# Seven products of quarters instead of eight in 39 weight blocks of a fused transformer kernel, and feed-forward groups of 6 and 4 tiles

## The chip, the core and the metric

The kernel runs on one core of a Trainium2 chip (trn2). A core has five engines with a queue each: TensorE (PE in the profile) multiplies matrices, VectorE (DVE) and ScalarE (ACT) work on elements, GpSimd (POOL) too, and SyncE (SP) issues most of the DMA transfers. Every engine does its own instructions in the order in which they were written, and the engines wait for each other through semaphores. The metric is the time of one execution on the device, in microseconds; the median of three runs was 2053.11 us (2051.51 to 2055.26).

## The reference

One transformer block of width 1024 over 512 tokens, then a second block that reads its output. All is fp32. What matters here are the three feed-forward networks, one in the first block ("ff" below) and two in the second ("ff1", "ff2"):

```python
def rmsnorm(x, g):
    y = x * lax.rsqrt(jnp.mean(x * x, axis=-1, keepdims=True) + EPS)
    return y * g

def swiglu(h, w1, w3, w2):
    return (jax.nn.silu(h @ w1) * (h @ w3)) @ w2

# first block: attention of two kinds with gates, then
h = rmsnorm(x, norm_mlp_g)
x = x + jnp.square(jax.nn.relu(h @ w_ff1)) @ w_ff2            # 1024 -> 4096 -> 1024   ("ff")
x = x + sigmoid(rmsnorm(x, norm_ple_g) @ w_ple_gate) * (p @ w_ple)
x = rmsnorm(x, final_norm_g)
# second block
x = x + 0.5 * swiglu(rms_norm(x, norm_ffn1), w1, w3, w2)      # 1024 -> 2816 -> 1024   ("ff1")
x = x + hybrid_mixer(rms_norm(x, norm_mix), ...)              # retention and differential attention
x = x + memory_attention(rms_norm(x, norm_mem_q), mem_n, ...)
x = x + 0.5 * swiglu(rms_norm(x, norm_ffn2), w1, w3, w2)      # ("ff2")
return rms_norm(x, norm_out)
```

## The kernel before

**Three matmuls for one product.** Each fp32 operand is split into two numbers that TensorE takes in one pass: `hi`, the value rounded to the format fp32r, and `lo`, the rest. A product is then three matmuls that add up in a PSUM bank, hi·hi, lo·hi and hi·lo (lines L612, L615, L618, where the weight is the stationary operand; L621, L624, L627, where the tokens are). Activations lie feature by feature: a tile is 128 features by 512 tokens, and a matmul of a weight tile (128x128) with it is 512 columns wide.

**Blocks.** All weights pass in blocks of 256 columns by 8 row tiles, 1 MB, through two buffers in turn (`b % 2`). For block b SyncE transfers the raw weights into `RAW[b % 2]` (`sp_weights`, L665) as soon as the block two before it has given up that buffer; ScalarE rounds them, chunk by chunk of 512 numbers for each partition, into `WH[b % 2]` (`act_weights`, L643), and VectorE subtracts to give the rest in `WL[b % 2]` (`dve_weights`, L652). An ordinary block has 4 chunks and 48 matmuls (2 output tiles, 8 row tiles, 3 each).

**The feed-forward networks.** `plan_ffn` cuts the hidden features into groups of 8 tiles (the last of ff1 and ff2 has 6). A "way up" block makes two hidden tiles of w1 (or w3); a "way down" block takes one group's hidden tiles times 256 columns of w2. All ways up of a group stand in a row, then the four ways down of the group before it. There are 60 blocks on the way up: 16 in ff, 22 in ff1, 22 in ff2. Each tile that comes out of PSUM is scaled by the row norm `RB` on VectorE (L1602 in ff with the relu; L1632 and L1637 in ff1 and ff2, where GpSimd multiplies once more, L1660), goes through ScalarE (L1615, or L1649 for silu), is rounded (L1618, L1653) and subtracted (L1607, L1641). What comes out of a way down is added to X on VectorE (L1571, L1573). The last group of ff2 is done with the tokens as the stationary operand, from weights that are fetched apart (`sp_late`, `act_late`, `dve_late`).

**What sets the order.** Each helper is a generator that yields a place (a block number with a fraction) ahead of its instructions; `weave` puts the instructions of all helpers of an engine into one queue by place. The order is so fixed when the kernel is built; a place is no time, and what an instruction really waits for are its semaphores.

## Time and profile before

| | |
|---|---|
| median of 3 runs | 2053.11 us (2051.51 to 2055.26) |
| the profiled execution | 2052.9 us |
| its span, first to last instruction | 2051.1 us |
| TensorE busy | 2035.3 us, 99% of the span |
| VectorE / ScalarE / GpSimd busy | 1171.7 / 858.3 / 307.6 us |
| granted TensorE clock, mean | 0.999 of full speed |
| DMA | 196 MB, 29.2% of 16 engines' time on the main queue |

How to read it: the profiler records start and end of each instruction. The ends of matmuls are modelled, and they are pipelined, so the mean duration of a matmul is longer than the distance from one to the next; the pace is read from the starts. A busy share of a whole span is a mean over stages. In a timeline a row is start, duration, engine, line, operation, what it writes and reads (m for SBUF, ps for PSUM), and in brackets how long the engine sat idle before it and who ended that.

### The profile page before, as it was taken

What the parts mean: (1) busy time and instruction counts of PE and PEld (TensorE: products, weight loads), DVE (VectorE), ACT (ScalarE), POOL (GpSimd) and SP (SyncE); (2) the same over time, 40 slices, a digit from 0 to 9 for tenths busy, and PEclk for the clock granted to TensorE, in tenths of its full rate; (3) what the DMA queues carried; (4) which work ended last, traced back from release to release, by engine and by line L of the source; (5) the groups of instructions that cost most, each with busy time, mean ns of one, the idle gap of its engine ahead of it and who ended that gap; (6) DMA issues with size and microseconds to landing.
All of it is one profiled execution on the core that took longest, in us unless ns stands there. A gap on an engine that the chain in (4) does not pass through costs nothing.

```text
span 2051.1 us, 26651 instructions
## 1 busy us (share of the span) xinstructions
PE 2035.3 (99%) x10420; PEld 1715.5 (84%) x10420; DVE 1171.7 (57%) x2237; ACT 858.3 (42%) x1631; POOL 307.6 (15%) x494
## 2 busy tenths in 40 slices
PE   9999999999999999999999999999999999999998
PEld 8788898888888888888888889978898888888887
DVE  7876557675434444675443545676876664544454
ACT  6666344454423233553322324555554443332332
POOL 0230000031000001131110103422551011110100
PEclk9999999999999999999999999999999999999999
DMA  6141422222332233222332223222342122332421
GB/s 193 44 154 42 126 83 85 69 96 85 111 103 98 88 103 103 83 95 91 103 103 87 99 83 108 94 68 93 106 151 83 62 76 89 103 103 90 157 72 42
DMA packets 193654, 195.98 MB, mean 96 GB/s; under 512 B 4844, under 2 KB 188460, under 8 KB 193452
## 3 DMA queue, kind: packets, MB, share of 16 engines
q1 hardware_dynamic: 192808, 193.22, 29.2%
q8 instruction: 83, 1.36, 0.3%
q10 hardware_dynamic: 720, 1.05, 0.1%
q14 instruction: 43, 0.35, 0.1%
HBM read 192.05 MB, written 6.93 MB: 97 GB/s over the span
## 4 chain that ended last, share of the span: by engine, by line
PE 93%; DVE 3%; POOL 1%; issue 1%; ACT 1%; DMA 0%; SPq 0%; DVEq 0%; POOLq 0%; ACTq 0%
PE ps L612 25%; PE ps L618 25%; PE ps L615 25%; PE ps L621 3%; PE ps L624 3%; PE ps L627 3%; PE ps L1145 1%; PE ps L1443 1%; DVE m L652 1%; PE ps L1452 1%; PE ps L1927 0%; DMA m<-xT 0%; PE ps L1155 0%; PE ps L1156 0%; PE ps L1157 0%
## 5 line engine op out<-in xcount | busy, mean ns | idle before, releaser
L612 PE MATMUL ps<-m,m 128*128 128x512 f32 x2336 | 919.8, 394 | 1.1 <-DVE m L941 0.8
L618 PE MATMUL ps<-m,m 128*128 128x512 f32 x2336 | 910.6, 390 | 0.2 <-DVE m L947 0.2
L615 PE MATMUL ps<-m,m 128*128 128x512 f32 x2336 | 909.6, 389 | 0.0
L643 ACT ACTIVATE m<-m 128x512 fp32r<-128x512 f32 x664 | 385.8, 623 | 554.9 <-PE ps L618 515.8
L652 DVE TENSOR_TENSOR m<-m,m 128x512 fp32r<-128x512 f32 x664 | 495.3, 764 | 51.7 <-ACT m L643 48.0
L618 PEld LDWEIGHTS ps<-m,m 128*128 128x128 f32 x2336 | 438.4, 188 | 93.8 <-DVE m L947 1.3
L612 PEld LDWEIGHTS ps<-m,m 128*128 128x128 f32 x2336 | 438.9, 188 | 90.5 <-issue 2.1
L615 PEld LDWEIGHTS ps<-m,m 128*128 128x128 f32 x2336 | 439.0, 188 | 87.4 <-DVE m L652 0.4
L621 PE MATMUL ps<-m,m 128*128 128x256 f32 (+1 forms) x566 | 168.5, 298 | 0.0
L624 PE MATMUL ps<-m,m 128*128 128x256 f32 (+1 forms) x566 | 164.7, 291 | 0.5 <-DVE m L652 0.5
L627 PE MATMUL ps<-m,m 128*128 128x256 f32 (+1 forms) x566 | 164.5, 291 | 0.0
L1660 POOL TENSOR_TENSOR m<-m,m 128x512 f32<-128x512 f32 x44 | 76.1, 1730 | 485.4 <-DVE m L1637 485.4
L704 POOL TENSOR_TENSOR m<-m,m 128x512 f32<-128x512 f32 x35 | 47.9, 1370 | 511.4 <-ACT m L688 511.1
L1571 DVE TENSOR_TENSOR m<-m,ps 128x512 f32<-128x512 f32 x56 | 38.5, 687 | 128.4 <-PE ps L618 128.4
L624 PEld LDWEIGHTS ps<-m,m 128*128 128x128 f32 x566 | 108.1, 191 | 3.0 <-DVE m L652 0.9
L621 PEld LDWEIGHTS ps<-m,m 128*128 128x128 f32 x566 | 108.1, 191 | 2.9 <-issue 0.4
L627 PEld LDWEIGHTS ps<-m,m 128*128 128x128 f32 x566 | 107.9, 191 | 1.7
L1632 DVE TENSOR_TENSOR m<-ps,m 128x512 f32<-128x512 f32 x44 | 30.3, 691 | 103.3 <-PE ps L618 103.3
L1573 DVE SCALAR_TENSOR_TENSOR m<-ps,m 128x512 f32<-128x512 f32 x40 | 27.6, 691 | 105.0 <-PE ps L618 105.0
L1653 ACT ACTIVATE m<-m 128x512 fp32r<-128x512 f32 x44 | 27.9, 633 | 121.9 <-POOL m L1660 121.9
L1637 DVE TENSOR_TENSOR m<-m,ps 128x512 f32<-128x512 f32 x44 | 30.3, 688 | 78.4 <-PE ps L618 78.4
L1602 DVE SCALAR_TENSOR_TENSOR m<-ps,m 128x512 f32<-128x512 f32 x32 | 22.1, 692 | 59.9 <-PE ps L618 59.9
(342 smaller groups left out, 1900.8 us busy)
## 6 DMA issues: line engine op xcount, KB each, us to landing
m<-ffn_w SPq DMA_DIRECT2D x60, 1024.0 KB, 5.1
m<-w_ff SPq DMA_DIRECT2D x32, 1024.0 KB, 5.0
m<-w_in SPq DMA_DIRECT2D x28, 1024.0 KB, 5.0
m<-w_in SPq DMA_DIRECT2D x17, 512.0 KB, 5.1
m<-w_out SPq DMA_DIRECT2D x8, 1024.0 KB, 4.8
m<-mem_w_kv SPq DMA_DIRECT2D x8, 1024.0 KB, 5.5
m<-w_out_a SPq DMA_DIRECT2D x4, 1024.0 KB, 4.7
m<-w_ple_gate SPq DMA_DIRECT2D x4, 1024.0 KB, 4.7
```

Source lines behind the costliest of these rows:

```text
L612: pe.matmul(o, lh, xh, start=k == 0, stop=False)
L615: pe.matmul(o, ll, xh, start=False, stop=False)
L618: done = pe.matmul(o, lh, xl, start=False, stop=k == nk - 1)
L621: pe.matmul(o, xh, wh[:, k, c:c + job.width], start=k == 0, stop=False)
L624: pe.matmul(o, xh, wl[:, k, c:c + job.width], start=False, stop=False)
L627: done = pe.matmul(o, xl, wh[:, k, c:c + job.width], start=False, stop=k == nk - 1)
L643: act.activation(self.WH[b % 2][:, at], self.RAW[b % 2][:, at], ACT.Copy).then_inc(*self.up("w_hi", b, c))
L652: dve.tensor_tensor(self.WL[b % 2][:, at], self.RAW[b % 2][:, at], self.WH[b % 2][:, at].bitcast(F32), ALU.subtract).then_inc(*self.up("w_ ...
L704: pool.tensor_tensor(self.ACC[:, :], self.ACC[:, :], self.tmp[t % 2], ALU.add).then_inc(*self.up("acc", v, t))
L1571: dve.tensor_tensor(x, x, self.bank(name), ALU.add).then_inc(*self.drained(name))
L1632: dve.tensor_tensor(slot, self.bank(up0), self.RB[:, :], ALU.mult).then_inc(*self.drained(up0))
L1660: pool.tensor_tensor(slot, slot, self.RB[:, :], ALU.mult).then_inc(*self.up("h_sum", name, t))
```

## The change

Of the 60 ways up, 39 (12 in ff, 14 in ff1, 13 in ff2) are computed by Strassen's scheme in Winograd's form. The weight block (1024 x 256) is cut into four quarters (512 x 128) and the activations (1024 x 512) into four quarters (512 features x 256 tokens). Seven products of sums of quarters take the place of eight products of quarters. Each product is 4 row tiles, three matmuls each, 256 columns wide: 84 matmuls of 256 columns stand for 48 of 512.

- Weights: VectorE makes four sums of quarters, written over the raw weights where it can (`m1`, `m3`, `m2`, `m4`), and there are 7 chunks to round and subtract instead of 4. Chunks 4 to 6 lie in an additional buffer `WX`.
- Activations: before the first such block of a network four sums of quarters are made, rounded and subtracted once (`act_split_x`, `dve_split_x`), from a copy of X with the gain in it.
- Outputs: the products gather in three banks, X, Z and W. Bank X goes on adding, and ScalarE copies it out at three points (`p1`, `u2`, `vc`; the matmuls of chunks 2, 4 and 6 wait for them); VectorE forms the four quarters of the result from banks and copies.
- No two split blocks stand side by side. Groups have 6 or 4 tiles, and ways up and down alternate one by one, so that between most split blocks lies one way down of 36 (or 24) matmuls of 512 columns. More groups also mean more results that are added to X: 32 more VectorE additions. The last group of ff2 has 4 tiles instead of 6.

Between one split block and the next stand, in 20 cases, one way down of 6 tiles; in 7, one of 4 tiles (3 in ff, 4 in ff1); in 5, one ordinary way up; in 4, two or three ways down.

The core of the diff:

```diff
-    def __init__(self, strips, nk, width, jobs, hold=0.0, together=False, end=None, late=False):
+    def __init__(self, strips, nk, width, jobs, hold=0.0, together=False, end=None, late=False, split=None):
         self.strips, self.nk, self.width, self.jobs = strips, nk, width, jobs
         self.hold, self.together, self.end = hold, together, end or jobs[-1].name
-        self.chunks, self.late = -(-nk * width // 512), late
+        self.chunks, self.late, self.split = 7 if split else -(-nk * width // 512), late, split
...
+        for n in {"ff": (6, 4, 4, 6, 6, 6), "ff1": (6, 4, 6, 6), "ff2": (6, 6, 6, 4)}[name]:
+            groups.append((t0, n))
+            t0 += n
...
+            order = []
+            while ups_of or before:
+                order += ups_of[:1] + (before[:1] if not (last and end and ups_of) else [])
+                before = before[1:] if not (last and end and ups_of) else before
+                ups_of = ups_of[1:]
...
+                    split = at - self.start[name, "up", 0] > {"ff": 4, "ff1": 5, "ff2": 3}[name] and (not self.splits or at - self.splits[-1] > 1)
...
+            if blk.split:
+                yield from self.pe_split(pe, new, b, blk)
+                continue
...
+        work = [("X", 0, quarter(0, 0), 0, 12, "s1"), ("Z", 1, made(2), 0, 8, None), ("X", 2, made(1), 0, 12, "s6"), ("Z", 1, made(2), 8, 12, "s7"),
+                ("W", 3, quarter(1, 0), 0, 4, None), ("X", 4, made(0), 0, 12, "s5"), ("W", 3, quarter(1, 0), 4, 12, "w"),
+                ("X", 6, quarter(1, 1), 0, 12, "x"), ("Z", 5, made(3), 0, 12, "z")]
...
+                    copied = {2: [self.at("scalar", "p1", b)], 4: [self.at("scalar", "u2", b)], 6: [self.at("scalar", "vc", b)],
+                              5: [self.at("vector", "c11", b)]}.get(c, [])
+                    for w in new(self.at("w_hi", b, c), *copied):
+                        pe.wait_ge(*w)
...
+                done = pe.matmul(out[half], weight[step == 1][c][:, k, :], xl if step == 2 else xh, start=a == 0 and c in (0, 1, 3), stop=a == 11 and c in (3, 5, 6),
+                                 skip_group_check=c != 3)
+            if event in ("x", "z", "w"):
+                done.then_inc(*self.full(("s" + event, b)))
+            elif event:
+                done.then_inc(*self.up("tensor", event, b))
...
+        return (a00, a01, a10, a11), [a00, a10, a00, a01, self.s1[:, :].rearrange("p (k c) -> p k c", k=4), a11, a01]
...
+    SPLIT_HI = (-0.92, -0.78, -0.6, -0.42, -0.2, 0.05, 0.41)
+    SPLIT_LO = (-0.8, -0.62, -0.45, -0.28, -0.05, 0.17, 0.48)
...
+            summed = {1: "m3", 2: "m2", 4: "m1", 6: "m4"}.get(c)
+            for w in new(self.at(f"w_in{b % 2}", b), *self.split_free(b, c), *([self.at("vector", summed, b)] if summed else [])):
+                act.wait_ge(*w)
+            act.activation(self.split_slot(b, c, 0), src[c], ACT.Copy).then_inc(*self.up("w_hi", b, c))
...
+        dve.tensor_tensor(s1, a10, a11, ALU.add).then_inc(*self.up("vector", "m1", b))
+        dve.tensor_tensor(a10, a00, a10, ALU.subtract).then_inc(*self.up("vector", "m3", b))
+        yield b + self.SPLIT_LO[0]
+        low(0)
+        yield b + self.SPLIT_LO[0] + 0.07
+        for w in new(self.at("vector", "m1", b), self.at("vector", "m3", b), self.at("w_lo", b, 0)):
+            dve.wait_ge(*w)
+        dve.tensor_tensor(a00, s1, a00, ALU.subtract).then_inc(*self.up("vector", "m2", b))
+        for c in (1, 2, 3):
...
+        dve.tensor_tensor(a01, a01, a00, ALU.subtract).then_inc(*self.up("vector", "m4", b))
+        for c in (4, 5, 6):
+            yield b + self.SPLIT_LO[c]
+            low(c)
...
+        t1, t2, t3, t4 = (self.split_x(n) for n in range(4))
+        step = 0.15 if name == "ff1" else 0.1
+
+        def low(n):
+            for w in new(self.at("scalar", "t_hi", name, n)):
+                dve.wait_ge(*w)
+            dve.tensor_tensor(self.TX[1][n], self.split_x(n), self.TX[0][n].bitcast(F32), ALU.subtract).then_inc(
...
+        for place, key, event, out in ((0.16, "p1", "s1", self.snap[0]), (0.39, "u2", "s6", self.snap[1]), (0.63, "vc", "s5", self.snap[2])):
+            yield b + place
+            for w in new(self.at("tensor", event, b), *([read[key]] if read else [])):
+                act.wait_ge(*w)
+            act.activation(out, X, ACT.Copy).then_inc(*self.up("scalar", key, b))
...
+            last = b - 2 + self.SPLIT_LO[6] + 0.06 if self.plan[b - 2].split else self.chunk_place(b - 2, self.plan[b - 2].chunks + 1) if b > 2 else -0.5
+            yield -1.0 if b == 1 else last
...
+            dve.tensor_tensor(s1[:, 256:512], z, vc, ALU.add).then_inc(*self.up("vector", "c11", b))
+            yield b + 0.75
+            for w in new(self.at("scalar", "p1", b), self.filled(("sw", b)), *self.slot_free("ff", t)):
+                dve.wait_ge(*w)
+            dve.tensor_tensor(s0[:, 0:256], w00, p1, ALU.add).then_inc(*self.drained(("sw", b)))
+            yield b + 0.82
+            for w in new(self.cleared(("sw", b)), self.rb_made("mlp")):
+                dve.wait_ge(*w)
+            dve.scalar_tensor_tensor(out=s0[:, 0:256], in0=s0[:, 0:256], scalar=0.0, in1=rb[:, 0:256], op0=ALU.max, op1=ALU.mult).then_inc(
+                *self.up("vector", "half", "ff", 0, t))
+            yield b + 0.9
+            for w in new(self.filled(("sx", b))):
+                dve.wait_ge(*w)
+            dve.scalar_tensor_tensor(out=s0[:, 256:512], in0=x01, scalar=0.0, in1=rb[:, 256:512], op0=ALU.max, op1=ALU.mult).then_inc(
+                *self.drained(("sx", b)))
+            yield b + 1.04
+            for w in new(self.filled(("sz", b)), self.at("scalar", "u2", b)):
+                dve.wait_ge(*w)
+            dve.tensor_tensor(s1[:, 0:256], z, u2, ALU.add).then_inc(*self.drained(("sz", b)))
+            yield b + 1.08
+            for w in new(self.cleared(("sz", b))):
+                dve.wait_ge(*w)
+            dve.scalar_tensor_tensor(out=s1, in0=s1, scalar=0.0, in1=rb[:, :], op0=ALU.max, op1=ALU.mult).then_inc(
+                *self.up("vector", "up", "ff", 0, t + 1))
+        elif not split:
...
-        return self.start["ff2", "dn", 1] + 0.4 + 0.25 * c
+        return self.start["ff2", "dn", 2] + 1.0 + 0.25 * c
```

**TensorE**, at an ordinary way up of ff before: m_49 and m_50 are the activations' hi and lo, m_53/m_54 and m_55/m_56 the weights' hi and lo buffers. A row is line, operation, out<-in, size of the output and the semaphores waited for.

```order
L612 MATMUL ps<-m_49,m_53 128x512 [waits w_hi,free1]
L615 MATMUL ps<-m_49,m_55 128x512 [waits w_lo]
L618 MATMUL ps<-m_50,m_53 128x512
L612 MATMUL ps<-m_49,m_53 128x512
L615 MATMUL ps<-m_49,m_55 128x512
```

and at the passage from the first to the second product of a split block now (m_188, m_189, m_193 are sums of activations; the semaphore "scalar" tells of a copy or a rounding, "vector" of a subtraction):

```order
L700 MATMUL ps<-m_49,m_54 128x256
L700 MATMUL ps<-m_49,m_56 128x256
L700 MATMUL ps<-m_50,m_54 128x256
L700 MATMUL ps<-m_189,m_54 128x256 [waits scalar,w_hi,free4]
L700 MATMUL ps<-m_189,m_56 128x256 [waits w_lo]
L700 MATMUL ps<-m_193,m_54 128x256 [waits vector]
L700 MATMUL ps<-m_189,m_54 128x256
L700 MATMUL ps<-m_189,m_56 128x256
L700 MATMUL ps<-m_193,m_54 128x256
L700 MATMUL ps<-m_189,m_54 128x256
```

The rows are half as wide, and among them stand waits for ScalarE's copies.

**VectorE**, in ff before, from one output tile on (L652 is a rest of weights, L1602 scales an output, L1607 is a rest of the hidden tile):

```order
L652 TENSOR_TENSOR m_56<-m_52,m_54 128x512 [waits w_hi]
L1607 TENSOR_TENSOR m_166<-m_191,m_158 128x512 [waits h_hi]
L1602 SCALAR_TENSOR_TENSOR m_192<-ps,m_61 128x512 [waits h_lo,full4]
L652 TENSOR_TENSOR m_55<-m_51,m_53 128x512 [waits w_hi] x2
L1607 TENSOR_TENSOR m_167<-m_192,m_159 128x512 [waits h_hi]
L652 TENSOR_TENSOR m_55<-m_51,m_53 128x512 [waits w_hi]
L1602 SCALAR_TENSOR_TENSOR m_190<-ps,m_61 128x512 [waits h_lo,full5]
```

and now from `m1` of a split block on, where the block before it is a way down of 4 tiles (L778, L779, L785, L792 are the sums of weights, L772 their rests, L728 rests of the neighbouring block, L1784 adds a way down to X, L1872 is the last step of the outputs of the split block before, L1835 the rest of a hidden tile):

```order
L778 TENSOR_TENSOR m_197<-m_52 128x512 [waits w_in1]
L779 TENSOR_TENSOR m_52<-m_52 128x4x128
L1872 SCALAR_TENSOR_TENSOR m_183<-m_183,m_61 128x512 [waits free4]
L772 TENSOR_TENSOR m_56<-m_52,m_54 128x512 [waits w_hi]
L1835 TENSOR_TENSOR m_178<-m_182,m_172 128x512 [waits h_hi]
L785 TENSOR_TENSOR m_52<-m_197,m_52 128x4x128 [waits w_lo,vector]
L772 TENSOR_TENSOR m_56<-m_52,m_54 128x512 [waits w_hi]
L1835 TENSOR_TENSOR m_179<-m_183,m_173 128x512 [waits h_hi]
L1784 TENSOR_TENSOR m_68<-m_68,ps 128x512 [waits full6]
L772 TENSOR_TENSOR m_56<-m_52,m_54 128x512 [waits w_hi] x2
L792 TENSOR_TENSOR m_52<-m_52 128x4x128 [waits w_lo,vector]
L772 TENSOR_TENSOR m_196<-m_197,m_195 128x512 [waits w_hi]
```

From L778 to the last of the seven L772 stand 17 operations (the twelve rows here are 13 of them; L1784, L772, L728 and L772 follow), then one L728, and then five operations of 256 elements on the outputs (L1850 to L1868) before the next L778.

**ScalarE**, in ff before (L643 rounds weights, L1615 squares, L1618 rounds):

```order
L1615 ACTIVATE m_191<-m_191 128x512 [waits free6]
L1618 ACTIVATE m_179<-m_191 128x512 [waits squared]
L643 ACTIVATE m_53<-m_51 128x512 x3
L1615 ACTIVATE m_192<-m_192 128x512 [waits free0]
L1618 ACTIVATE m_180<-m_192 128x512 [waits squared]
L643 ACTIVATE m_54<-m_52 128x512 [waits full1,w_in1]
L1615 ACTIVATE m_190<-m_190 128x512 [waits free1]
L1618 ACTIVATE m_181<-m_190 128x512 [waits squared]
```

and now, from the first chunk of a split block to its third copy (L762 rounds a sum of weights, L719 a chunk of the neighbouring block, L865 copies bank X):

```order
L762 ACTIVATE m_195<-m_197 128x512
L719 ACTIVATE m_53<-m_51 128x512 [waits full2,w_in0]
L762 ACTIVATE m_195<-m_52 128x512 [waits full6]
L865 ACTIVATE m_198<-ps 128x256 [waits free0,tensor]
L719 ACTIVATE m_53<-m_51 128x512
L865 ACTIVATE m_199<-ps 128x256 [waits free6,tensor]
L762 ACTIVATE m_195<-m_52 128x512 [waits vector,full5]
L865 ACTIVATE m_200<-ps 128x256 [waits tensor]
L1888 ACTIVATE m_182<-m_182 128x512 [waits free3,vector]
```

The copies stand between roundings of two blocks.

## Rows read from the trace of the kernel before

**Rows 1.** The page: its head, busy time by engine, granted TensorE clock in 40 slices.

```profile
span 2051.1 us, 26651 instructions
PE 2035.3 (99%) x10420; PEld 1715.5 (84%) x10420; DVE 1171.7 (57%) x2237; ACT 858.3 (42%) x1631; POOL 307.6 (15%) x494
...
PEclk9999999999999999999999999999999999999999
```

**Rows 2.** The page, part 4: the chain that ended last, by engine.

```profile
PE 93%; DVE 3%; POOL 1%; issue 1%; ACT 1%; DMA 0%; SPq 0%; DVEq 0%; POOLq 0%; ACTq 0%
```

**Rows 3.** Groups by line and shape, TensorE: count, busy us, mean ns, idle before.

```profile
L612 PE MATMUL ps<-m,m 128*128 128x512 f32 x2336 | 919.8, 394 | 1.1 <-DVE m L941 0.8 <-ACT m L905 0.3
...
L621 PE MATMUL ps<-m,m 128*128 128x256 f32 x524 | 151.8, 290 | 0.0
```

**Rows 4.** Timeline, TensorE, 512-wide stretch: start us, duration us; 55 matmuls, first and last.

```profile
499.64 0.39 PE L618 MATMUL ps<-m,m 128*128 128x512 f32 x1
...
511.88 0.39 PE L618 MATMUL ps<-m,m 128*128 128x512 f32 x1
```

**Rows 5.** Timeline, TensorE, 256-wide stretch: 12 matmuls, first and last.

```profile
1454.32 0.28 PE L621 MATMUL ps<-m,m 128*128 128x256 f32 x1
...
1455.63 0.28 PE L627 MATMUL ps<-m,m 128*128 128x256 f32 x1
```

**Rows 6.** Timeline, TensorE, 256-wide behind four 128-wide transposes.

```profile
1459.95 0.36 PE L621 MATMUL ps<-m,m 128*128 128x256 f32 x1
1460.15 0.28 PE L624 MATMUL ps<-m,m 128*128 128x256 f32 x1
```

**Rows 7.** Windows inside the three networks: length, then busy us of PE, PEld, DVE, ACT, POOL.

```profile
500.00:820.00 320.00, 320.00 (x1414) 265.05 (x1413) 140.68 (x213) 108.70 (x189) 5.36 (x4) 1.00 0.31 101
930.00:1240.00 310.00, 310.00 (x1369) 256.70 (x1368) 147.17 (x204) 91.93 (x160) 38.24 (x24) 1.00 0.29 95
1700.00:1980.00 280.00, 280.00 (x1237) 231.83 (x1236) 130.72 (x181) 87.43 (x153) 36.46 (x21) 1.00 0.33 111
...
1673.00:1695.00 22.00, 21.83 (x101) 17.92 (x100) 12.48 (x30) 9.37 (x17) 2.68 (x2) 1.00 0.33 96
```

**Rows 8.** Groups by line and shape, VectorE.

```profile
L1496 DVE TENSOR_TENSOR m<-ps,m 128x768 fp32r<-128x768 f32 x16 | 15.3, 957 | 16.5 <-ACT m L1516 16.5
...
L2164 DVE TENSOR_TENSOR m<-ps,m 128x256 f32<-128x256 f32 x4 | 1.7, 418 | 0.5 <-PE ps L2129 0.5
```

**Rows 9.** The same, ScalarE.

```profile
L1244 ACT ACTIVATE m<-ps 128x256 f32<-128x256 f32 x1 | 0.4, 364 | 0.0
```

**Rows 10.** Timeline, ScalarE and VectorE at a block's weights: runs of four and three.

```profile
765.33 2.20 ACT L643 ACTIVATE m<-m 128x512 fp32r<-128x512 f32 x4 [8.68 <-PE ps L618]
765.99 1.90 DVE L652 TENSOR_TENSOR m<-m,m 128x512 fp32r<-128x512 f32 x3
```

**Rows 11.** Timeline, from a last matmul to its reader.

```profile
759.40 0.39 PE L618 MATMUL ps<-m,m 128*128 128x512 f32 x1
...
759.83 0.69 DVE L1571 TENSOR_TENSOR m<-m,ps 128x512 f32<-128x512 f32 x1 [2.82 <-PE ps L618]
```

**Rows 12.** Timeline, from VectorE to the matmul that waits for it.

```profile
1456.10 0.68 DVE L2082 TENSOR_TENSOR m<-m,m 128x512 fp32r<-128x512 f32 x1
...
1456.83 0.50 PE L2127 MATMUL ps<-m,m 128*128 128x512 f32 x1 [0.92 <-DVE m L2082]
```

**Rows 13.** Timeline, from the last rest of a block's weights to the next transfer.

```profile
564.60 0.68 DVE L652 TENSOR_TENSOR m<-m,m 128x512 fp32r<-128x512 f32 x1
...
565.30 0.37 SPq L665 DMA_DIRECT2D m<-w_ff  x1
```

**Rows 14.** The page, part 6: transfers of 1 MB, KB each, us to landing.

```profile
m<-ffn_w SPq DMA_DIRECT2D x60, 1024.0 KB, 5.1
```

**Rows 15.** Line L652, VectorE: duration ns min/median/max.

```profile
L652 DVE TENSOR_TENSOR m<-m,m x664: 668/686/1792, 5.6 to 1991.9; 128x512 fp32r<-128x512 f32 x166
```

**Rows 16.** Line L1660, GpSimd: duration ns min/median/max.

```profile
L1660 POOL TENSOR_TENSOR m<-m,m x44: 1667/1705/1803, 914.6 to 1964.9; 128x512 f32<-128x512 f32 x44
```

418 lines of the change are left out of this document (316 added, 102 removed).

## The prediction

> **What bounds the kernel now.** I read the page's head first: TensorE is busy for 2035.3 of 2051.1 us at the full clock in all 40 slices [rows 1], and 93% of the chain that ended last is TensorE's [rows 2]. So time is won only by fewer or faster matmuls, and the other engines matter only where they make one late. Their room stands in the windows of the three networks: VectorE 140.7 of 320 us, 147.2 of 310 and 130.7 of 280 (44 to 47%), ScalarE 30 to 34% [rows 7]; TensorE has no gap there.
>
> Next the pace. The 394 and 290 ns of the groups [rows 3] are modelled durations that overlap; the starts give the price. 512-wide: 54 distances in 511.88 - 499.64 = 12.24 us, 0.2267 us each [rows 4]. 256-wide: 11 distances in 1.31 us, 0.1191 us each [rows 5]. Half the width costs 53% of the time.
>
> **TensorE's part.** An ordinary way up is 48 x 0.2267 = 10.88 us. A split one is 84 x 0.1191 = 10.00 us. Seven eighths of 10.88 would be 9.52; the narrow shape gives back 0.48. 39 blocks x 0.876 = 34.2 us less. The ways down have as many matmuls of the same shape as before, regrouped (6 tiles: 36 x 0.2267 = 8.16 us, 4 tiles: 5.44). Break-even would be a pace of 10.88 / 84 = 0.1295.
>
> The trace has a restart cost: behind four narrow transposes the first 256-wide matmul is followed after 0.20 instead of 0.12 us [rows 6]. A split block is 256 wide throughout, with no narrow ones, so I charge nothing in it. The other bound is 0.08 us for each of the nine pieces: 0.72 x 39 = 28 us.
>
> In the Trainium skill, "TensorE: Matmul & The Clock Gate", section "LDWEIGHTS (loading the stationary operand)", a load takes its number of columns over 1.2 GHz, 107 ns for 128, and the section on the back-to-back gap says the spacing is set by both operations. If load and matmul came one behind the other, 84 x (0.107 + 0.119) = 19 us would make a split block far slower, an estimate from that page. The 0.1191 us between 256-wide matmuls that each have a load of their own says they overlap, and the trace decides.
>
> **VectorE's added work.** Operations of 512 from SBUF last 0.686 us [rows 15], but three in a run take 1.90 us [rows 10], so they start (1.90 - 0.69) / 2 = 0.60 apart. A split block has 7 rests and 4 sums instead of 4 rests, +7 x 0.60, and outputs of five 256-operations (0.418 [rows 8], 0.33 at the same overlap) and one of 512 instead of two of 512, +1.05: +5.25 us. 39 blocks: 205 us; the 32 more additions to X 19 us; the sums of activations, 3 x 8 operations of 1024 (957 ns at 768 and 418 at 256 [rows 8] give 1.23 at 1024), 28 us. VectorE goes from 44 to about 65% there; on average that hides. Order is what can hurt, in two places.
>
> **The loop through the raw buffer.** The transfer for a split block b+2 starts when the last rest of b is made; its first operation needs the landing. Count from the start of b, with a way down of 4 tiles between (15.44 us from split to split). Chunk six is rounded behind copy `u2`. That follows matmul 32: 31 x 0.119 + 0.28 + 0.04 [rows 11] = 4.0. Copy 0.36 [rows 9], rounding 0.62, rest 0.69: 5.8. Transfer issued 0.02 later [rows 13], lands after 5.1 [rows 14]: 10.9. From there VectorE has 17 operations to the last rest of b+2: 10.3 at 0.60, so 21.2, that is 5.8 into b+2, the same phase as before. Its matmul waits for it at 61 x 0.119 = 7.3. So the tightest cycle closes with 1.5 us to spare. With 6 tiles between (20 cases) 2.72 us come on top against one more operation. If instead every operation took 0.72 (0.69 and a wait), the 7 short cycles would lose 2.0 us each, 14 us at most. The trace shows three in a run at 0.60; I take that and keep 14 for the range.
>
> **The copies.** Three times in each block a matmul waits for a ScalarE copy of bank X, covered by 8 matmuls of another bank. Last matmul's start to next use: 9 x 0.119 = 1.07. In it: 0.28 to its end, 0.04 to the reader [rows 11], 0.364 copy [rows 9], 0.05 back to TensorE [rows 12] = 0.73. Cover left: 0.34 us. That is less than one rounding of 0.62 (in a run of four (2.20 - 0.62) / 3 = 0.53 apart [rows 10]), so a copy that finds one just begun costs up to 0.28. Two stand ahead of the first copy in the order. In the short cycle of ff ScalarE's queue from the landing (the squaring waits until 12.8 for VectorE's third operation; two operations to 14.2, four roundings to 16.3, the neighbour's chunk 16.8, chunk five 17.4, copy 17.7) ends 0.1 before its need at 15.44 + 20 x 0.119 = 17.8: free. In ff1 a GpSimd operation of 1.7 us [rows 16] comes ahead of the hidden tile's rounding: about 0.3 late, in two of four cycles. I take 2 us for all copies; bounds 0 and 39 x 3 x 0.28 = 33.
>
> **The rest.** The first two blocks of each network carry the sums of activations: about 9.5 us more on VectorE, in 22 us where it is busy for 12.5 (ff2's start, the last window of [rows 7]). Rests are made half a block early, which covers a delay of some 3 us; I take 1 us for all three, bounds 0 and 3 x 3. At the end, a token tile's last products take 24 x 0.2267 = 5.4 us instead of 8.2; the tail behind the last matmul is as before. Its late weights are fetched in 4 pieces one after the other; bounds -2 and +3, I take 0.
>
> Sum: 2052.9 (profiled execution) - 34.2 + 2 + 1 = 2021.7. The median of the runs is 0.2 above that execution: **2022 us**.
>
> **The rivals.**
> - *The forecast, most of it hidden* (2017 to 2031). For it: the paces are read, and the tightest cycle closes on paper. Against: 1.5 and 0.34 us of cover are little in 39 blocks. Chance 0.70.
> - *VectorE's loop binds*: 0.72 for each operation, 14 us, and ordinary weights late at the networks' starts, 4: 2036. For it: the order puts waits for ScalarE ahead of nearly each rest. Chance 0.09.
> - *The port between VectorE and GpSimd.* L652 has a median of 686 ns and a maximum of 1792 [rows 15], 1.1 us more, and GpSimd's own L1660 1.7 us [rows 16]. In the ten split blocks of w3 two GpSimd operations run where VectorE now has eleven SBUF operations for four; each may cost 1.1 us in the loop: 22 us if nothing covers them, 2022 + 22 = 2044. Against: 6-tile cycles have over 2 us of room. Chance 0.05. The Trainium skill, "SBUF — State Buffer", section "Who interferes with whom", has this rule: a VectorE operation with two SBUF inputs and a GpSimd operation that reads SBUF lock each other out for a whole instruction. By that rule, the trace agrees: the 1.1 us.
> - *Matmuls in pieces do not hold 0.119*: +28 us as above (2050). Only rows behind narrow ones speak for it. Chance 0.07.
> - *Slower: the copies.* The place is ScalarE's queue ahead of `p1`, `u2`, `vc`. If the first finds two roundings ahead (0.53 + 0.62 - 0.34 = 0.8) and each other one (0.3), a block loses 1.4 us, 55 us: 2022 + 55 = 2077. The gain is gone from 0.88 us a block on, that is from a mean delay of 0.29 for each copy. For it: in-order queues, and chunk six, ahead of `vc`, waits for a VectorE sum. Against: ScalarE is at a third now and goes to about half. Chance 0.09.
>
> **How the numbers follow.** 0.2% is 4.1 us, about what a measurement of this kernel can tell from no change. The first three cases lie below 2049 (0.84). Of the matmul case half is a gain and half none, of the copies' case a quarter each is a gain and none: faster 0.89, same 0.06, slower 0.05. The range runs from 2016 (no stall and a shorter end) to 2042: it leaves out the port at full price and the two dear cases, about 2 in 10.
>
> **What would show it.** The split blocks' matmuls should start 0.119 us apart, a block from first to first in 10.0 us; TensorE's busy time should fall by about 34 us and its idle time grow by little. Idle time ahead of the matmul line put down to ScalarE's copies prices the copies; to VectorE's rests, the loop. VectorE should stand near 65% in the networks. Wrong would be: 256-wide starts above 0.13 apart, gaps of 0.3 us or more three times in a block, or rests landing behind matmul 61.

## The result and the profile after

The changed kernel takes 2033.09 us (median; 2029.00 to 2035.69) beside 2054.19 for the kernel before: ratio 0.9897, 95% interval 0.9877 to 0.9917. In a second series it took 2031.08 beside 2054.97, 0.9891 (0.9877 to 0.9906). It is 1.0 to 1.1% faster, two thirds to three quarters of the forecast gain (2022 us, -32): the time lies inside the range, 11 us above the forecast. The profiled execution took 2035.69 us, its span 2033.9.

The page after: head, busy times, granted clock, and from part 4 the chain.

```profile
span 2033.9 us, 30582 instructions
PE 2011.0 (99%) x11818; PEld 1761.5 (87%) x11818; DVE 1438.3 (71%) x2722; ACT 992.6 (49%) x1901; POOL 302.0 (15%) x494
...
PEclk9999999999999999999999999999999999999999
...
PE 87%; DVE 5%; DMA 2%; POOL 2%; ACT 2%; issue 2%; SPq 0%; DVEq 0%; POOLq 0%; ACTq 0%
```

Against [rows 1, 2]: TensorE has 1398 more matmuls in 24.3 us less, VectorE 267 us more, and 6% of the chain left TensorE. From part 5: the split matmuls, ScalarE's copies, the roundings of weight sums.

```profile
L700 PE MATMUL ps<-m,m 128*128 128x256 f32 x3276 | 400.6, 283 | 4.3 <-ACT m L865 4.3
...
L762 ACT ACTIVATE m<-m 128x512 fp32r<-128x512 f32 x273 | 163.5, 623 | 131.1 <-DMA m<-ffn_w 58.9
L772 DVE TENSOR_TENSOR m<-m,m 128x512 fp32r<-128x512 f32 x273 | 188.1, 699 | 43.6 <-ACT m L762 42.5
...
L865 ACT ACTIVATE m<-ps 128x256 f32<-128x256 f32 x117 | 44.7, 382 | 97.8 <-PE ps L700 97.8
```

The first row holds the main reading: in all 3276 split matmuls TensorE waited 4.3 us, every time for a copy. The windows of the three networks (as [rows 7]) show where:

```profile
500.00:820.00 320.00, 317.89 (x1874) 283.48 (x1873) 227.75 (x372) 150.03 (x270) 5.34 (x4) 1.00 0.32 99
930.00:1240.00 310.00, 307.79 (x1907) 277.98 (x1906) 242.96 (x380) 137.64 (x255) 39.50 (x26) 1.00 0.31 99
1700.00:1980.00 280.00, 280.00 (x1750) 254.18 (x1749) 212.10 (x336) 123.68 (x231) 30.25 (x21) 1.00 0.32 104
```

In these windows TensorE has gaps of 2.1 us in ff and 2.2 us in ff1, and none at all in ff2, although VectorE is busy there for 76%.

To say where time went, I cut each profile at the first matmul of the sums of squares that opens each network (in the changed kernel L931 at 488.35 for ff, L931 at 834.11 behind it, L2092 at 896.43 for ff1, L931 at 1244.55, L931 at 1674.67 for ff2) and at the last matmul (2025.42). "First" runs up to the start of the first attention product, L1222 at 51.58. "ff1 net" is ff1 without what TensorE lost in its first 15 us against its steady pace: 1.7 us in profiles with a stretch at half clock there (last section), 0.6 to 0.8 in the others. "Late" is the time that the split blocks of ff and of ff1 took beyond 10.07 us each, the length of an undisturbed one. All in us; each row is one profiled execution, each ratio is to the kernel before in the same series. The stretches left out differ by under 0.5 us.

| kernel | first | ff | ff1 | ff1 net | ff2 | late: ff, ff1 | behind last matmul | ratio to before (95%) |
|---|---|---|---|---|---|---|---|---|
| before | 47.35 | 352.33 | 354.70 | 353.9 | 361.06 | - | 7.06 | 1 |
| changed | 51.58 | 345.76 | 348.12 | 346.4 | 350.75 | 2.8, 2.9 | 8.46 | 0.9897 (0.9877-0.9917) |
| changed, again | 46.58 | 345.38 | 347.93 | 347.3 | 350.75 | 2.4, 3.8 | 8.44 | 0.9891 (0.9877-0.9906) |
| no_split | 49.45 | 352.32 | 356.16 | 354.4 | 360.89 | - | 8.47 | 1.0009 (1.0000-1.0018) |
| narrow_96 | 46.67 | 360.24 | 365.39 | 363.7 | 369.47 | - | 8.41 | 1.0139 (1.0125-1.0153) |
| narrow_84 | 46.39 | 342.97 | 345.20 | 343.5 | 350.75 | 0, 0 | 8.44 | 0.9866 (0.9852-0.9879) |
| copies_first | 49.32 | 345.34 | 347.65 | 345.9 | 350.75 | 2.4, 2.4 | 8.45 | 0.9890 (0.9874-0.9905) |
| transfer_later | 46.96 | 344.11 | 348.03 | 346.3 | 350.75 | 1.2, 2.8 | 8.47 | 0.9890 (0.9875-0.9905) |
| early_free | 49.55 | 344.10 | 349.53 | 347.8 | 350.77 | 1.1, 4.4 | 8.45 | 0.9904 (0.9888-0.9921) |
| no_pool | 48.72 | 345.37 | 345.12 | 343.4 | 350.74 | 2.4, 0.4 | 8.48 | 0.9888 (0.9873-0.9902) |
| pool_later | 48.98 | 345.36 | 347.90 | 346.2 | 350.78 | 2.4, 2.7 | 8.46 | 0.9891 (0.9876-0.9906) |
| copies_transfer | 49.67 | 343.88 | 346.63 | 346.0 | 350.75 | 0.9, 2.5 | 8.44 | 0.9891 (0.9874-0.9907) |
| new_tail | 49.33 | 345.63 | 348.40 | 346.7 | 350.74 | 2.7, 3.2 | 7.98 | 0.9897 (0.9882-0.9911) |
| best | 48.93 | 344.25 | 345.50 | 344.9 | 350.74 | 1.3, 1.4 | 8.39 | 0.9878 (0.9863-0.9893) |

The ratios of the eight small variants can't be told apart. The stages can: where an edit touches nothing in it, ff lies between 345.36 and 345.76, ff1 net between 346.4 and 347.3 (three profiles), ff2 within 0.04 us. What is smaller than that spread I don't count.

### The profile page after: what moved, and what is told of

It reads as the page before. It is cut to its first block, busy times and chain, and to the rows that moved or that the text cites. A ratio compares the mean times of both kernels' runs of the same rounds, so it can differ in the third digit from the quotient of the medians.

```text
span 2033.9 us, 30582 instructions
## 1 busy us (share of the span) xinstructions
PE 2011.0 (99%) x11818; PEld 1761.5 (87%) x11818; DVE 1438.3 (71%) x2722; ACT 992.6 (49%) x1901; POOL 302.0 (15%) x494
## 3 DMA queue, kind: packets, MB, share of 16 engines
q10 hardware_dynamic: 720, 1.05, 0.1%
## 4 chain that ended last, share of the span: by engine, by line
PE 87%; DVE 5%; DMA 2%; POOL 2%; ACT 2%; issue 2%; SPq 0%; DVEq 0%; POOLq 0%; ACTq 0%
PE ps L637 18%; PE ps L643 17%; PE ps L640 17%; PE ps L700 17%; PE ps L646 3%; PE ps L649 3%; PE ps L652 3%; DMA m<-w_ff 1%; DMA m<-w_in 1%; PE ps L1358 1%; DVE m L728 1%; ACT m L762 1%; PE ps L1656 1%; PE ps L1665 1%; DMA m<-ffn_w 1%
## 5 line engine op out<-in xcount | busy, mean ns | idle before, releaser
L637 PE MATMUL ps<-m,m 128*128 128x512 f32 x1728 | 685.5, 397 | 2.2 <-ACT m L1118 1.4
L643 PE MATMUL ps<-m,m 128*128 128x512 f32 x1728 | 675.3, 391 | 0.2 <-DVE m L1160 0.2
L640 PE MATMUL ps<-m,m 128*128 128x512 f32 x1728 | 674.9, 391 | 0.0
L719 ACT ACTIVATE m<-m 128x512 fp32r<-128x512 f32 x512 | 306.7, 623 | 245.9 <-PE ps L643 202.9
L700 PEld LDWEIGHTS ps<-m,m 128*128 128x128 f32 x3276 | 398.6, 192 | 8.4 <-ACT m L762 4.1
L700 PE MATMUL ps<-m,m 128*128 128x256 f32 x3276 | 400.6, 283 | 4.3 <-ACT m L865 4.3
L728 DVE TENSOR_TENSOR m<-m,m 128x512 fp32r<-128x512 f32 x512 | 379.7, 758 | 26.9 <-ACT m L719 26.0
L643 PEld LDWEIGHTS ps<-m,m 128*128 128x128 f32 x1728 | 325.1, 188 | 71.6 <-DVE m L1160 1.6
L637 PEld LDWEIGHTS ps<-m,m 128*128 128x128 f32 x1728 | 325.6, 188 | 67.2 <-ACT m L1118 1.8
L640 PEld LDWEIGHTS ps<-m,m 128*128 128x128 f32 x1728 | 325.9, 189 | 62.2 <-DVE m L728 0.3
L762 ACT ACTIVATE m<-m 128x512 fp32r<-128x512 f32 x273 | 163.5, 623 | 131.1 <-DMA m<-ffn_w 58.9
L772 DVE TENSOR_TENSOR m<-m,m 128x512 fp32r<-128x512 f32 x273 | 188.1, 699 | 43.6 <-ACT m L762 42.5
L646 PE MATMUL ps<-m,m 128*128 128x256 f32 (+1 forms) x548 | 162.8, 297 | 0.0
L649 PE MATMUL ps<-m,m 128*128 128x256 f32 (+1 forms) x548 | 159.0, 290 | 0.7 <-DVE m L728 0.7
L652 PE MATMUL ps<-m,m 128*128 128x256 f32 (+1 forms) x548 | 158.7, 290 | 0.0
L1992 POOL TENSOR_TENSOR m<-m,m 128x512 f32<-128x512 f32 x44 | 70.7, 1607 | 538.9 <-DVE m L1959 279.1
L917 POOL TENSOR_TENSOR m<-m,m 128x512 f32<-128x512 f32 x35 | 47.9, 1369 | 462.3 <-ACT m L901 462.1
L649 PEld LDWEIGHTS ps<-m,m 128*128 128x128 f32 x548 | 105.4, 192 | 3.0 <-DVE m L728 1.6
L646 PEld LDWEIGHTS ps<-m,m 128*128 128x128 f32 x548 | 105.5, 193 | 2.4 <-issue 0.4
L652 PEld LDWEIGHTS ps<-m,m 128*128 128x128 f32 x548 | 105.3, 192 | 1.1
L1784 DVE TENSOR_TENSOR m<-m,ps 128x512 f32<-128x512 f32 x72 | 49.3, 685 | 65.9 <-PE ps L643 65.9
L865 ACT ACTIVATE m<-ps 128x256 f32<-128x256 f32 x117 | 44.7, 382 | 97.8 <-PE ps L700 97.8
```

Of the source, the lines that this page charges most:

```text
L637: pe.matmul(o, lh, xh, start=k == 0, stop=False)
L640: pe.matmul(o, ll, xh, start=False, stop=False)
L643: done = pe.matmul(o, lh, xl, start=False, stop=k == nk - 1)
L646: pe.matmul(o, xh, wh[:, k, c:c + job.width], start=k == 0, stop=False)
L649: pe.matmul(o, xh, wl[:, k, c:c + job.width], start=False, stop=False)
L652: done = pe.matmul(o, xl, wh[:, k, c:c + job.width], start=False, stop=k == nk - 1)
```

## Three kernels that split the gain: no_split, narrow_96, narrow_84

```diff
-                    split = at - self.start[name, "up", 0] > {...}[name] and (...)
+                    split = False
```

> No block is split: the 39 ways up are ordinary again (48 matmuls of 512), and the sums of the activations are gone; the groups of 6 and 4, the alternation one by one and the new last group stay. My theory: the regrouping alone is worth nothing but the later tail, +1.4 us, so 2055 to 2057 us (ratio to the kernel before 1.000 to 1.001), and the whole gain of the changed kernel is that of the split blocks. Rival A: the regrouping itself costs 4 us or more (32 more additions on VectorE, 16 to 24 more narrow weight blocks), then 2059 us or above and the split blocks gain 25 or more. Rival B: the regrouping gives part of the gain, then 2050 us or below.

It came out as the theory had it: 1.0009, tail 8.47. The regrouping wins nothing and costs the tail's 1.4 us; ff and ff2 are within 0.2 us of before; ff1 is 1.5 longer, 0.5 net.

```diff
+            steps = ... if b not in self.narrow else [(job, h, None, k) for job in blk.jobs for h in range(2) for k in range(8)]
...
+                    at = slice(256 * n, 256 * n + 256) if b in self.narrow else job.tokens
```

> As the kernel without split blocks, but the same 39 ways up run their ordinary product in 96 matmuls of 256 columns instead of 48 of 512. My theory: a matmul of 256 columns costs 0.1199 us here, as in the split blocks, whatever is around it: 96 x 0.1199 = 11.51 us per block against 10.90, +0.61 x 39 = +23.8 us over the kernel without split blocks, about 2079 to 2081 us. Rival: the 0.1199 in place of 0.1191 is the price of the split blocks' many waits and mixed banks; then 96 x 0.1191 = 11.43, +20.8 us over the kernel without split blocks.

The theory's 23.8 us was nearly right: the three networks together are 25.7 us longer than in no_split, and the median, 2083.00 us, lies 2 us above the forecast. The starts inside the narrow blocks are 0.1199 us apart (3705 distances, mean), as in split blocks, and not the 0.1191 of [rows 5]; so neither the waits nor the mixed banks of Strassen's form cost pace. The rest is new: the 512-wide matmuls of the networks now start 0.2270 to 0.2273 us apart on average, in no_split 0.2267 to 0.2268. The single distances show where this comes from: only the first five behind each narrow block are longer (on average 233, 235, 229, 232 and 231 ns), and from the sixth on they are 226.7 ns as before. In the changed kernel the sixth matmul behind a split block starts 1.16 us after the first instead of 1.13:

```profile
1747.29 0.40 PE L637 MATMUL ps<-m,m 128*128 128x512 f32 x1
...
1748.45 0.39 PE L643 MATMUL ps<-m,m 128*128 128x512 f32 x1
```

A narrow stretch behind 512-wide matmuls is the other way round: it starts with distances of 113 or 114 and 119 ns and then goes on at 120.

```diff
-                ... for k in range(8)]
+                ... for k in range(8) if not (h and k in (3, 5))]
```

> As the one with 96 narrow matmuls, but 12 of the 96 are left out in each of the 39 blocks (part of the sums over features is missing): TensorE has exactly the split blocks' 84 matmuls of 256 columns, while no copies, no sums of quarters and only four chunks per block stand on the other engines. My theory: 39 x 12 x 0.1199 = 56.1 us below the 96; and what the changed kernel stands above it is what copies, sums and their stalls cost, 5.6 us of stalls and perhaps 1.6 us at the start of the second network: so 2024 to 2028 us. Rival: the work on the other engines costs nothing beyond its stalls being replaced by others, then within 2 us of the changed kernel (2031 to 2035).

The 12 matmuls less are worth 56.2 us in the three networks (narrow_96's 1095.10 to 1038.92; 39 x 12 x 0.1199 = 56.1). The changed kernel stands above this one by 2.8 us in ff, 2.9 in ff1 (net too) and 0.01 us or less in ff2. That is the full price of all copies, sums and seven chunks, 5.7 us, and its split blocks' lateness sums to the same 5.7. Its second profile has 2.4 and 3.8, 6.2 us in all, again equal to the lateness of its blocks. The same place in both kernels, first matmul of a narrow block and of the next block. The changed kernel:

```profile
1737.22 0.28 PE L700 MATMUL ps<-m,m 128*128 128x256 f32 x1
...
1747.29 0.40 PE L637 MATMUL ps<-m,m 128*128 128x512 f32 x1
```

and the kernel without copies and sums:

```profile
1725.97 0.28 PE L639 MATMUL ps<-m,m 128*128 128x256 f32 x1
...
1736.05 0.40 PE L639 MATMUL ps<-m,m 128*128 128x512 f32 x1
```

10.07 and 10.08 us: where it is not late, Strassen's form is free of charge beside its 84 matmuls.

## The stalls in ff: copies_first, transfer_later, early_free, copies_transfer

The changed kernel stalls in six blocks of 39, five times for `p1`, once for `u2`. The first, in the timeline (start us, us; in brackets the idle time before and what ended it):

```profile
577.64 0.69 DVE L772 TENSOR_TENSOR m<-m,m 128x512 fp32r<-128x512 f32 x1 [2.23 <-ACT m L762]
...
578.36 1.00 SPq L878 DMA_DIRECT2D m<-w_ff  x2
...
584.76 0.69 DVE L778 TENSOR_TENSOR m<-m 128x512 f32<-128x512 f32 x1 [1.39 <-DMA m<-w_ff]
...
587.90 2.27 ACT L762 ACTIVATE m<-m 128x512 fp32r<-128x512 f32 x4
...
590.08 0.61 ACT L719 ACTIVATE m<-m 128x512 fp32r<-128x512 f32 x1
...
590.60 0.61 ACT L762 ACTIVATE m<-m 128x512 fp32r<-128x512 f32 x1
...
591.12 0.36 ACT L865 ACTIVATE m<-ps 128x256 f32<-128x256 f32 x1
...
591.62 2.62 PE L700 MATMUL ps<-m,m 128*128 128x256 f32 x20 [0.86 <-ACT m L865]
```

Read it from the top: the last rest of split block b frees the raw buffer at 578.33, two transfers are issued at once (b+2's 1 MB and, 0.6 us later, its neighbour's 512 KB), the first lands after 6.4 us instead of 5.1 [rows 14], six roundings stand ahead of `p1`, and the matmul starts 1.02 us beyond its pace (0.86 us behind the modelled end of the one before).

```diff
-    SPLIT_HI = (-0.92, -0.78, -0.6, -0.42, -0.2, 0.05, 0.41)
+    SPLIT_HI = (-0.92, -0.78, -0.6, -0.42, -0.2, 0.2, 0.41)
-    SPLIT_LO = (-0.8, -0.62, -0.45, -0.28, -0.05, 0.17, 0.48)
+    SPLIT_LO = (-0.8, -0.62, -0.45, -0.28, -0.05, 0.25, 0.48)
...
+        if self.plan[b - 1].split:
+            return b - 1 + 0.18 + 0.66 * c / (self.plan[b].chunks + 1)
```

> The changed kernel with another order on ScalarE and VectorE: the first copy p1 of bank X stands ahead of the rounding of chunk five and of the neighbour's first chunk (place of chunk five 0.05 to 0.2, its rest 0.17 to 0.25, the chunks of the block after a split one from 0.18 on). My theory: the five waits of TensorE for p1 (0.53 to 1.05 us each, 4.1 us with what follows them 4.4) come from ScalarE's order; they shrink to what the late transfer leaves, 1 us in all: about 3 us faster than the changed kernel, near 2030 us, and only the wait for u2 at the first split of ff1 stays. Rival: the whole loop of the raw buffer is late in those cycles, so the waits only move to u2, to vc or to chunk five (no change within 1 us, 2032 to 2035).

The rival, for the short cycles: -0.4 us in ff at most, and ff1 net is 345.9, 0.5 below the lowest of the untouched profiles. What went is the one that the theory kept: the first split block of ff1, which waits for `u2`, is 0.5 us late instead of 1.3. TensorE's waits, in us, times and longest:

```profile
PE ps L700 <- DVE m L774: 0.8, 5, 0.2
PE ps L700 <- ACT m L867: 0.5, 2, 0.3
```

The copies are early enough now, but behind them TensorE waits for VectorE's rests (L772 before). Each such wait is split in two or three smaller ones that sum to nearly the old one.

```diff
-                for w in new(self.at("w_lo", b - 2, self.plan[b - 2].chunks - 1)):
+                for w in new(self.at("w_lo", b - 2, self.plan[b - 2].chunks - 1),
+                             *([self.at(f"w_in{(b - 1) % 2}", b - 1)] if self.plan[b - 1].split else [])):
```

> The changed kernel, but the transfer of an ordinary block that follows a split one is asked for only when the split block's own transfer has landed. My theory: in ff the split blocks' 1 MB in the three cycles with a way down of 4 tiles took 6.38, 5.89 and 5.92 us because the neighbour's 512 KB ran beside them; alone they take 5.1, so everything up to the first copy comes 0.8 to 1.3 us sooner and the three stalls of ff (1.09, 0.60, 1.12 us with their restart) vanish: ff from 345.8 to about 343.2 us between its first sum and the next stage's, ff1 (transfers of 5.3 us) unchanged at 348.1; the whole 2 to 2.5 us faster, near 2031. Rival: VectorE and ScalarE have too much queued in those cycles and the neighbour's chunks, now 2 to 3 us later, block them in their queues: the stalls stay or grow, 2033 to 2036.

In ff the theory, by half: two stalls gone but for 0.1 to 0.2 us, the third 0.6 (1.05 before), ff 1.3 to 1.6 us shorter (344.11) of 2.8; ff1 net as it was. The same transfer took 5.6 us instead of 6.4, in the three short cycles of ff 5.5 to 5.6 instead of 5.9 to 6.4:

```profile
573.76 6.00 SPq L879 DMA_DIRECT2D m<-w_ff  x2
...
579.34 0.69 DVE L778 TENSOR_TENSOR m<-m 128x512 f32<-128x512 f32 x1 [0.57 <-DMA m<-w_ff]
```

```diff
-    SPLIT_HI = (..., 0.05, 0.41)
+    SPLIT_HI = (..., -0.05, 0.18)
-    SPLIT_LO = (..., 0.17, 0.48)
+    SPLIT_LO = (..., 0.06, 0.26)
...
+        if self.plan[b - 1].split:
+            return b - 1 + 0.22 + 0.62 * c / (self.plan[b].chunks + 1)
```

> The changed kernel with the last two chunks of a split block rounded and subtracted sooner (roundings at -0.05 and 0.18 of the block instead of 0.05 and 0.41, rests at 0.06 and 0.26 instead of 0.17 and 0.48) and the neighbour's chunks 0.18 of a block later: the raw buffer comes free, and the next split block's transfer is asked for, some 2 us sooner. My theory: the loop around the raw buffer is what is late in the cycles with a way down of 4 tiles (15.4 us for 5.1 to 6.4 of transfer and 17 operations on VectorE); with 2 us more all of the five stalls for p1 go (4.4 us), the one at the first split block of ff1 stays (1.3): about 4 us faster, near 2029 us. Rival: VectorE's capacity in these cycles binds, not where the loop starts; then the stalls only change places, within 1 us of the changed kernel.

Neither wholly. ff fell to 344.10, the same as by the later transfer, so there it is the loop and not VectorE's capacity. ff1 net did not get shorter, 347.8 against 346.4 to 347.3: in two short cycles the stall moved from `p1` to `u2` (0.5 and 1.1 us), and at the first split block TensorE now waits 2.2 us for `u2`, since GpSimd's multiplication lasted 2.9 us there and ScalarE stood behind it.

> The two edits together: copies ahead of chunk five, and the neighbour's transfer behind the split block's. Alone they took ff from 345.8 to 345.3 and to 344.1 us, with one stall for p1 of 0.61 us left. My theory: with the transfer 0.8 to 1.3 us sooner VectorE is no longer late for what the copies uncovered, so ff falls to 343.0 to 343.4 us (343.0 is the time with the same matmuls and no copies or sums); ff1 347.5. Rival: the third cycle stays late on VectorE whatever the order, ff 344 us or more.

ff 343.88: 0.2 us better than the later transfer alone, 0.5 short of the theory. One stall (0.4 us for a rest, in the third short cycle) stays. In ff1 the 346.63 looks better than forecast, but this execution had no half clock there; net it is 346.0, 0.4 below the lowest of the untouched profiles and no more than copies_first had.

## The stalls in ff1: no_pool, pool_later

```diff
-        for w in new(self.at("h_sum", name, t), *self.h_before(name, g)):
+        for w in new(*self.up_read(name, 1, t), *self.h_before(name, g)):
-        s += [self.pool_swiglu(pool, new, name, v, t) for ...]
```

> The changed kernel without GpSimd's multiplication in ff1 and ff2 (the outputs of the gated networks lack that factor). My theory: in ff1 the three stalls (1.28 us at 960.5, 0.83 at 1063.1, 0.80 at 1095.0, with their restart) exist because GpSimd's L1992 holds back VectorE's strided subtraction (1.6 us instead of 0.7) and, at the first, ScalarE's L1985: they vanish, ff1 from 348.1 to 345.2 us between the marks, ff and ff2 unchanged, the whole about 2.9 us faster. Rival: they come from the late transfer and VectorE's queue as in ff; then at most 1 us of the 2.9 goes.

The theory: ff1 345.12, net 343.4, and narrow_84 had 345.20 and 343.5. The lateness of ff1's split blocks fell from 2.9 us to 0.4, so nearly all of it is GpSimd's; another 0.5 us went behind the last split block, where narrow_84 still has the multiplication. The changed kernel at the second of the three stalls:

```profile
1057.19 1.67 POOL L1992 TENSOR_TENSOR m<-m,m 128x512 f32<-128x512 f32 x1 [2.10 <-DVE m L1967]
1057.82 1.59 DVE L785 TENSOR_TENSOR m<-m,m 128x512 f32<-128x512 f32 x1
...
1059.44 0.63 ACT L762 ACTIVATE m<-m 128x512 fp32r<-128x512 f32 x1 [1.74 <-DVE m L785]
```

L785, means over ff1, with GpSimd's multiplication and without:

```profile
L785 DVE TENSOR_TENSOR m<-m,m 128x512 f32<-128x512 f32 x14 | 15.1, 1079 | 1.5
```

```profile
L785 DVE TENSOR_TENSOR m<-m,m 128x512 f32<-128x512 f32 x14 | 9.7, 693 | 1.5
```

```diff
+        late = [self.at("scalar", "p1", b + 2)] if name == "ff1" and t % 2 and ... else []
+        for w in new(*self.up_read(name, 1, t), self.rb_made(v), *late):
```

> The changed kernel, all its work kept: in ff1 GpSimd's multiplication of the odd tile of a split block of w3 waits for the first copy p1 of the next split block (with ScalarE's rounding and VectorE's rest of that tile moved behind it), and the rounding of hidden tile 5 stands behind u2 of the first split block. Without the multiplication at all ff1 took 345.1 us instead of 348.1. My theory: it is the place where it meets VectorE's subtraction m2 ahead of p1 that costs, so the three stalls go as they did without it: ff1 345.2 to 345.8 us, ff and ff2 unchanged. Rival: wherever it runs it holds VectorE as long, and VectorE has no room in the cycles with a way down of 4 tiles: at least two stalls stay, ff1 347 us or more.

The rival, for these cycles: ff1 347.90, net 346.2, 0.2 us below the lowest without the edit. The two old stalls for `p1` went and two others came, 1.1 us for `p1` at 1075 and 0.7 at 1098, where the block's last product waits for a sum of VectorE's (`c11`). The trace shows how it comes back:

```profile
1058.24 1.80 POOL L1993 TENSOR_TENSOR m<-m,m 128x512 f32<-128x512 f32 x1 [6.79 <-ACT m L865]
1058.80 1.79 DVE L772 TENSOR_TENSOR m<-m,m 128x512 fp32r<-128x512 f32 x1
...
1063.02 0.99 SPq L878 DMA_DIRECT2D m<-ffn_w  x2
...
1068.63 0.69 DVE L778 TENSOR_TENSOR m<-m 128x512 f32<-128x512 f32 x1 [1.88 <-DMA m<-ffn_w]
...
1075.08 1.19 PE L700 MATMUL ps<-m,m 128*128 128x256 f32 x8 [0.94 <-ACT m L865]
```

A rest is held back now (1.79 us instead of 0.69), the last rest follows later, so the next transfer does too, and the next block is late. In these cycles, with 1 us or so to spare, it did not matter where the 1.1 us fell. At the first split block the stall for `u2`, 1.2 us, gave way to one of 0.3 us for `c11`; that is the part of the edit that helped.

## The end, and all of it together: new_tail, best, the changed kernel again

```diff
+            if i == 2 and step:
+                yield self.last_place(7 if step == 1 else 8) + 0.15
...
+        if i == 2:
+            c = self.result[i][:, 0:SPLIT]
+            act.activation(c, c, ACT.Copy, scale=q["r"]).then_inc(*self.up("scalar", "result", i))
```

> The changed kernel with another order at the very end: of the chain of tiny operations for token tile 2 on VectorE, four stand where they stood, two behind the reads of unit 7 and two behind those of unit 8, and ScalarE instead of VectorE scales tile 2's first 640 columns. My theory: the end of the changed kernel is 1.4 us later than before (8.5 us behind the last matmul against 7.1) because this chain stands ahead of the reads of the last units; without that 7.1 to 7.4 us, so 1.1 to 1.4 us faster, 2032 us. Rival: the last transfers, not VectorE, set the end (they start 3.2 us before it): then 8.3 us or more stay.

Between the two: 0.5 us of the 1.4 (7.98). VectorE reads the last unit 0.70 us behind the start of the last matmul; in the changed kernel it was 1.71:

```profile
2027.13 0.42 DVE L2941 SCALAR_TENSOR_TENSOR m<-ps,m 128x256 f32<-128x256 f32 x1
```

but the two tiny operations left between that read and the last chain took back 0.4 us, and the order alone did not empty VectorE's queue.

> All of it together: copies ahead of chunk five, the later transfer of the neighbour, the later multiplication on GpSimd, and a new tail (ScalarE scales 640 columns of tiles 1 and 2, and of tile 2's tiny chain only two operations stand behind the reads of unit 7). My theory: ff 343.3, ff1 345.5, ff2 350.8, behind the last matmul 7.2 to 7.6 us instead of 8.5: 6 us faster than the changed kernel, a ratio to the kernel before of 0.987 (0.990 for the changed kernel). Rival: the edits take the same slack twice (the later chunks of the neighbour and the later rests of the hidden tile meet in VectorE's queue), then ff1 stays above 347 us and the gain is under 3 us.

ff 344.25 and ff1 net 344.9: 1.1 to 1.5 us less in ff and 1.5 to 2.4 in ff1 than the changed kernel's two profiles. (The 345.50 that I forecast for ff1 is met only because this execution had no half clock there.) In ff1 no edit that keeps all the work came more than 0.5 us below the best untouched profile by itself; with the copies first and the later transfer, GpSimd's later place does (346.0 to 344.9). Why it pays only then was not tried. The end failed, 8.39: six tiny operations ahead of unit 6 delayed its read by about 1 us, and VectorE never caught up. The whole takes 2029.31 us against the changed kernel's 2031.08, 1.8 us less where 6 were forecast; the intervals overlap, so the 2.6 us or more that the stages show are not shown by the runs' times.

> The changed kernel once more, beside the three others on the same chip. The first 52 us of the profile (the same instructions in all these kernels) took between 46.4 and 51.6 us in the eight profiles of kernels with the new groups and 47.4 in that of before: I take this for a difference between executions, so the profiled span of this run should lie within 2029 to 2034 us by the start alone, with ff 345.8, ff1 348.1, ff2 350.8 us within 0.5 us each. Rival: the changed kernel's start is later for a reason of its own; then it is again 51 us or more.

The theory: 46.58 us to the first mark, ff, ff1 and ff2 within 0.4 us. So the 4.2 us of the first profile's start are that execution's. Net, though, ff1 is 0.9 us longer here: the stalls at the short cycles took 1.07 and 1.09 us instead of 0.75 and 0.72. So single stages of one kernel differ by up to 1 us from one execution to the next.

## Why the prediction was right, and where it was off

The mechanism was right; four sizes were off. Working in spans, I had -31.2 us, the profile shows -17.2.

| term | forecast | measured | from |
|---|---|---|---|
| split blocks' TensorE time | -34.2 | -30.4 | narrow_84 less no_split |
| copies, sums, loop | +3 | +5.7 | changed less narrow_84; +6.2 in the second profile |
| regrouping | 0 | +1.3 | no_split less before (0.9 of it at ff1's start) |
| between the networks | 0 | +0.6 | marks |
| the end | 0 | +1.4 | marks |
| the first 52 us | 0 | +4.2 | marks; -0.8 in the second profile |

- **The pace.** The step from 11 distances in 1.31 us [rows 5] to a price took a stretch so short that its first distances, 113 and 119 ns, pull the mean down. Long stretches give 0.1199: 10.07 us a block, +2.7 us. The kernel before had one as well, 188 distances in 22.54 us:

```profile
1260.11 0.28 PE L621 MATMUL ps<-m,m 128*128 128x256 f32 x1
...
1282.64 0.28 PE L627 MATMUL ps<-m,m 128*128 128x256 f32 x1
```

  And I took the 512-wide pace of [rows 4] as fixed; behind each narrow block five distances are longer, about 25 ns together, which makes some 1.1 us over all. A break-even of 0.1295 made this harmless for the sign.
- **Nine pieces, no restart**: right. Blocks that nothing delays take 10.07 us; the 75 ns restart appears only behind a wait, as in [rows 6]. That rival is dead.
- **The loop through the raw buffer** was the right place with the wrong length in one link. I ended the last rest at 5.8 (the terms that I listed sum to 5.7); it ended at 5.66. I took a lone transfer's 5.1 us; it took 6.4. I had listed the transfer for b+2, but not that the neighbour's is issued 0.6 us behind it and runs beside it. `p1` was then done at 18.81 instead of 17.7, against a need of 17.9: the 0.1 us of cover became 1.0 us late here, 0.5 and 1.0 in the other two short cycles of ff. The Trainium skill, "DMA: Bandwidth & Descriptors", section "Rules for kernel authors", says that transfers share the same 16 engines whichever engine issues them; by that rule the two would slow each other here. The trace agrees in part: in the short cycles of ff a transfer took 5.85 to 6.38 us beside the neighbour's and 5.47 to 5.56 without it, in those of ff1 5.0 to 5.4 and 5.0 to 5.1. So the neighbour explains 0.3 to 0.9 us of the difference in ff; why even the undisturbed transfers there took 0.4 us more than 5.1 stays open.
- **VectorE's share** was forecast as 65% and is 71, 78 and 76%. Part is only counting: I added 0.60 a piece, and busy time counts 0.69. The 65% was also a wrong sum: the added 252 us on VectorE (24 operations of 1.23 us are 29.5 and not 28) come to about a quarter of the networks' 1030 us, and 44 to 47% plus that is about 70%. It never bound on average; ff2 at 76% lost nothing.
- **The copies**: 2 us forecast, 4.3 of waits and 5.7 in all measured, in five of the seven short cycles and at ff1's start. The order on ScalarE, which I gave as cause, is the smaller part (moved alone it gave 0.4 us at most in ff, copies_first); the lateness of everything behind the transfer is the larger (1.3 us or more, transfer_later and early_free).
- **The port.** I had it as a rival at 22 us and, in the forecast, as 0.3 us for a hidden tile's rounding. It is real and small: of ff1's 2.9 us of stalls 2.5, and none in ff2, where each block has the room of a 6-tile way down or of an ordinary way up. What VectorE lost was its own operation (L785, +0.9 us), not only the rounding, and at ff1's first split block GpSimd itself was stretched to 2.9 us.
- **The end.** "The tail is as before" was wrong: with 4 tiles in the last group a unit takes 2.7 us instead of 4.1, while VectorE's work for it stayed the same, so its backlog reaches past the last matmul. I had looked at TensorE's side of the shorter products only.

## What to carry to other kernels

When a scheme removes matmuls at the price of work elsewhere, build a version with the same matmuls and none of that work: here it gave 5.7 to 6.2 us of 30, and showed that one of the three networks paid nothing. A loop that closes with little to spare is judged with every transfer that runs at the same time, and with the other engine's lock wherever it may fall: moving the disturbance inside the loop gave nothing by itself, making the loop shorter gave 1.3 us or more in ff. A price read from a short stretch should be checked on the longest one that the trace has. A group made smaller to feed TensorE better also shortens the time in which others must finish behind it.
